# Two 32-byte paddings in SBUF: the moving operands of a matmul stream shifted against its weights

## The reference, cut to what matters

```python
p  = rmsnorm(x, norm_mix) @ w_in            # first block, then its three mixers
x  = x + concat([y_a, y_b, y_c]) @ w_out
up = dwconv3(rmsnorm(x, norm_ffn) @ ffn_w_up)
x  = x + (silu(gate) * val) @ ffn_w_down    # gate, val: the halves of up
proj = rms_norm(x, norm_g) @ w_in_2         # second block, then its three branches
mk, mv = split(rms_norm(mem) @ w_mem_kv)
merged = sigmoid(ga)*(ya @ w_up_a) + sigmoid(gb)*(yb @ w_up_b) + sigmoid(gc)*(yc @ w_up_c)
out = x + merged @ w_o
```

## The kernel before, in words

| tile | bytes from raw0 | modulo 128 before |
|---|---|---|
| raw, w_hi, w_lo (12 buffers of 4096) | 0 to 49151 | 0 |
| x (16384), par (2548), con (4368) | 49152, 65536, 68096 | 0 |
| h_hi, h_lo (16384 each) | 72480, 88864 | 32 |
| shared area | 105248 | 32 |

## Time and profile before

### The profile page before, as it was taken

The page is one execution under the profiler, slowest core; times in us unless marked ns, Lnnn a source line. Parts: engine busy times, 40 slices in busy tenths (PEclk is TensorE's granted clock), DMA queues, the critical chain, the costliest instruction groups (busy, mean ns, idle before and its releaser), DMA issues.

```text
span 2505.9 us, 51128 instructions
## 1 busy us (share of the span) xinstructions
PE 2418.7 (97%) x19960; PEld 2378.8 (95%) x19960; DVE 1533.2 (61%) x2050; ACT 1186.3 (47%) x1502; POOL 12.8 (1%) x27
## 2 busy tenths in 40 slices
PE   6999998999999999996899999999999999999999
PEld 6899998999999999996899999999999999999999
DVE  6556566666556666567866666776576454544454
ACT  5343335666435666434444445444465443433433
POOL 0000000000000000000000000000000000000000
PEclk9999898999999999998999999999999999999999
DMA  6353354555555555553333333333344365555554
GB/s 236 136 186 118 132 187 136 183 189 179 201 187 179 183 191 180 197 187 128 122 118 112 112 112 120 120 115 118 139 161 160 117 202 177 186 177 173 189 185 159
DMA packets 110145, 400.39 MB, mean 160 GB/s; under 512 B 12394, under 2 KB 12421, under 8 KB 109904
## 3 DMA queue, kind: packets, MB, share of 16 engines
q1 hardware_dynamic: 108000, 391.00, 46.7%
q0 software_dynamic: 2032, 7.67, 0.9%
HBM read 396.52 MB, written 2.10 MB: 159 GB/s over the span
## 4 chain that ended last, share of the span: by engine, by line
PE 91%; DVE 5%; issue 1%; ACT 1%; DMA 0%; DVEq 0%; SPq 0%; ACTq 0%
PE bank L417 90%; DVE w_lo L1316 1%; DVE scratch L1365 1%; ACT w_hi L909 1%; PE bank L611 1%; DVE h_lo L1362 0%; DVE s_k L1365 0%; DMA x<-in_xT 0%; DVE cum L1362 0%; DVE root L1404 0%; DVE ping L1362 0%; DVE s_t L1362 0%; DVE qr L1807 0%; DVE acc L1362 0%; DVE s_t L1369 0%
## 5 line engine op out<-in xcount | busy, mean ns | idle before, releaser
L1316 DVE TENSOR_TENSOR w_lo<-raw,w_hi 128x1024 fp32r<-128x1024 f32 x736 | 891.7, 1224 | 775.2 <-ACT w_hi L909 766.8
L909 ACT ACTIVATE w_hi<-raw 128x1024 fp32r<-128x1024 f32 x736 | 771.1, 1058 | 987.2 <-PE bank L417 966.9
L417 PE MATMUL bank<-h_hi,w_hi 128*128 128x256 f32 x4016 | 1151.1, 287 | 38.0 <-DVE h_lo L1362 15.9
L417 PE MATMUL bank<-h_lo,w_hi 128*128 128x256 f32 x4016 | 1128.2, 281 | 0.0
L417 PE MATMUL bank<-h_hi,w_lo 128*128 128x256 f32 x4016 | 1127.4, 281 | 0.0
L417 PEld LDWEIGHTS bank<-h_hi,w_hi 128*128 128x128 f32 x4016 | 762.5, 190 | 48.4 <-issue 22.4
L417 PEld LDWEIGHTS bank<-h_lo,w_hi 128*128 128x128 f32 x4016 | 762.6, 190 | 3.0 <-issue 1.9
L417 PEld LDWEIGHTS bank<-h_hi,w_lo 128*128 128x128 f32 x4016 | 761.8, 190 | 0.0
L417 PE MATMUL bank<-m_hi,w_hi 128*128 128x256 f32 x704 | 196.5, 279 | 0.0
L417 PE MATMUL bank<-m_lo,w_hi 128*128 128x256 f32 x704 | 196.5, 279 | 0.0
L417 PE MATMUL bank<-m_hi,w_lo 128*128 128x256 f32 x704 | 196.5, 279 | 0.0
(11 more groups left out here) (414 smaller groups left out, 2815.8 us busy)
## 6 DMA issues: line engine op xcount, KB each, us to landing
raw<-in_units SPq DMA_DIRECT2D x736, 512.0 KB, 3.4
x<-in_xT SPq DMA_DIRECT2D x4, 512.0 KB, 6.3
memx<-in_memT POOLq DMA_DIRECT2D x4, 512.0 KB, 7.0
out_y<-obuf SPq DMA_DIRECT2D x8, 256.0 KB, 4.1
bias_t<-in_bias POOLq DMA_DIRECT2D x8, 192.0 KB, 2.9
dft<-in_dft POOLq DMA_DIRECT2D x1, 1024.0 KB, 7.4
decay<-in_decay POOLq DMA_DIRECT2D x1, 768.0 KB, 5.5
con<-in_con SPq DMA_DIRECT2D x1, 546.0 KB, 8.5
```

The costliest lines, as they stand in the source:

```text
L417: return pe.matmul(out, lhsT, rhs, start=start, stop=stop, skip_group_check=True)
L909: return act.activation(out, in_, ACT.Copy, scale=scale)
L1316: dve.tensor_tensor(w_lo[slot][:, :, :], raw[slot][:, :, :], w_hi[slot][:, :, :].bitcast(F32), ALU.subtract).then_inc(split_done, 1)
```

## The change

Two tiles of 32 bytes that nobody reads or writes are allocated, one ahead of `h_hi` and one ahead of the shared area. `h_hi` and `h_lo` move up by 32 bytes, and everything in the shared area moves up by 64. `spare` is placed 768 bytes lower in the shared area, since behind it no room for the shift is left. By the sizes above, the h pair then starts at 72512 bytes, 64 modulo 128, and the shared area at 105312 bytes, 96 modulo 128; the weights, x, par and con stay. No instruction is added or taken away.

```diff
         con = sb("con", [P, NCONST])
+        sb("pad_h", [P, 8])
         h_hi = sb("h_hi", [P, KT, T], F32R)
         h_lo = sb("h_lo", [P, KT, T], F32R)
+        sb("pad_arena", [P, 8])
         arena_at = nc.sbuf_base
...
         K = 1024
-        spare = place("spare", [P, 8], 105 * K)
+        spare = place("spare", [P, 8], 106752)
```

## The result

The changed kernel takes 2526.84 us (2522.24 to 2535.75, 7 runs) against 2510.84 us (2504.41 to 2513.36, 7 runs) for the kernel before: ratio 1.0082, 95% interval 1.0065 to 1.0099. It is slower by 0.8%, which is 16 us between the medians and 21 by the ratio. The profiled executions differ by 2525.59 - 2507.54 = 18.05 us.

What follows compares the result with a forecast made beforehand. The prediction took the pace of TensorE's matmul stream to bound the kernel. Its terms, 0 + 0 + 0 and the two paces, gave 2507 us, own range 2500 to 2520, and 2496 to 2556 for 8 in 10.

Steps and rivals of the forecast that it cites:

- What bounds the kernel: Whole kernel: the pace of TensorE's matmul stream sets the time, with 91% of the chain on TensorE.
- Instructions, transfers, vector engines at 0: All queues, weight loads and conversions: nothing added or moved that costs time, 0, bound ±1.3 us for the vector engines.
- the remark that at half clock the distance does not matter: Matmuls at half clock: about 200 ns each, so a load of 188 ns fits inside whatever the distance.
- The matmul stream at 0 ns per matmul: All float32r matmuls: new distances between moving operand and weights cost 0 ns, bounds -5 and +3 ns, -86 to +52 us.
- the slower rival: Matmul stream: 64 or 96 is a worse distance, 3 ns per matmul, 2559 us, area alone 2524; chance 0.17.
- The first, full-float32 matmuls at two distances with equal times: Full-float32 matmuls of 256 columns: 215.5 ns at distance 32 and 215.2 at 0, taken as no effect, weak evidence.
- The second, the 3 ns between chains of 128 columns and transposes: Load-limited chains: 112 ns at distance 0, transposes 109 at 96; the difference need not be the distance.
- The third, regularity over steps of 512 bytes: Matmul stream: distances change in multiples of 512 bytes, yet all come at 116.7 or 117.7 ns.
- The small difference is not one of addresses: Feed-forward windows: paces 116.7 and 117.7 ns occur in the same loop at the same addresses, so addresses do not cause them.
- The faster rival: Matmul stream: 32 bytes is a bad distance costing some 5 ns; avoiding it gives 2421, 2447 or 2479 us; chance 0.15.
- Two read ports: TensorE: independent read ports for moving operand and weights, from a skill page; by it the sum is also 0.
- 109.2 ns: Matmul stream: a skill page's estimate for 256 columns, N / 2.4 + 2.5 ns, against 116.7 in the trace; 2378 us.

Runs made afterwards that it cites:

- all_up32: The kernel before with 32 bytes of padding ahead of the first buffer, so weights and everything behind move up by 32: ratio 0.9994, 2505.73 us.
- h448_a448: The change's two paddings at other sizes, h and the shared area both at 448 modulo 512 from the weights: ratio 0.9818 to the kernel before, 2462.87 us.
- w_up96: The kernel before with w_hi and w_lo moved by 96 bytes and everything behind them by 512: ratio 0.9873, 2474.81 us.
- w_lo_up96: The kernel before with only w_lo moved by 96 bytes and what lies behind by 512: one run, 2538.47 us against 2503.27.
- h_lo_up64: The kernel before with only h_lo moved by 64 bytes, the shared area kept at 288 modulo 512: one run, 2513.96 us against 2508.75.
- short_loads: The changed kernel with 64 instead of 128 weight columns in two of three matmuls of unit(): one run, 2517.73 us.
- short_moves: The changed kernel with 128 instead of 256 moving columns in two of three matmuls of unit(): 3263.83 us.

## Why the prediction was wrong, point by point

**What bounds the kernel:** right. TensorE's stream was 91% of the chain and is 92% of it; each nanosecond per matmul appeared in the time nearly in full (20 us worked out below, 18.05 measured).

**Instructions, transfers, vector engines at 0:** right. The conversions kept 1224 and 1058 ns, and the busy times of both engines agree within 0.6 us. So was the remark that at half clock the distance does not matter (last section).

**The matmul stream at 0 ns per matmul:** this is the step that failed. The distance of moving operand and weights sets the pace, and the term is not 0. The measured terms are +3.3 ns in y and m (116.7 to 120.0), +2.3 in ya and mg (mostly 117.7 before), and for h +1.0 where it had been at 116.7, against -3.3 in a few units. As an estimate over the units of the two profiles: y and m 2880 x 3.3 = 9.5 us, ya and mg 1920 x 2.2 = 4.2, mh some 2, and h some 239 units more at 117.7 for 6 us less 25 units at 113.3 for 2. The sum is 20 us, where the profiles differ by 18.05. In y and m the term is even beyond the upper bound of +3 that the prediction set. The parts measured alone point the same way: 0.5% with the area at 96 and h untouched, 0.17% with both at 64. They do not add up to the change strictly, since the second moves the area as well; h alone at 64 was not tried.

**The numbers:** the likeliest time, 2507, and its own range of 2500 to 2520 rest on the 0. The wide range, up to 2556, takes in the measured 2526.84 only because most of the slower rival was put into it, and that rival had 0.17.

**Why the reasons for 0 did not hold.** The first, full-float32 matmuls at two distances with equal times, was called weak and was: in the profiles of eleven kernels, over which the float32r stream went from 113.3 to 120.0, `gsq,con` stayed between 215.5 and 216.0 ns. The second, the 3 ns between chains of 128 columns and transposes, was none of distance; the transposes went from 96 to 32 and stayed at 0.60 us for four. The third, regularity over steps of 512 bytes, was correct as an observation, and the prediction named the loophole itself, a conflict in the lowest bits that are constant over the stream. I gave that loophole too little. Some 5 ns lay unexplained between what the rows of parts allow and what the stream takes, and at 192 most of them go (113.3). They were the hint that the distance costs something; once it does, there is no reason for the present distance to be neutral.

**"The small difference is not one of addresses":** right, and it misled me. One place has two paces, and in the feed-forward block of all_up32 and of h448_a448 each half keeps one of them from its start to its end. That was taken as evidence against an effect of the place. But the place sets which two paces there are.

**The rivals.** The slower one came true in its place, the area, and in its size there; that load and moving read meet more often, as it says, no run shows. Its time for the area alone, 2524, is near the measured time, partly by luck, since h lost some 4 us too and the kernel before was 3.7 us above 2507 beside the changed one; its 3 ns for every matmul, 2559, is what h at 96 and the area at 0 came near to (2548.87). The faster rival was wrong for this change and right for its neighbours: with both at 192 modulo 256 the stream gains 3.3 ns per matmul where it draws the quick pace, 2462.87 us, and the rival gave 2421 to 2479.

**Two read ports, and 109.2 ns.** The section "Who interferes with whom" of the Trainium skill's page "SBUF — State Buffer" has the two read ports of TensorE independent and nothing but the port shared by VectorE and GpSimd as a source of contention. For the time, the runs disagree: moving the weights alone by 96 bytes took 1.3% off the kernel (w_up96). They do not show that it is the ports that clash. The 109.2 ns that the prediction worked out from "Back-to-back issue gap" (the Trainium skill, "TensorE: Matmul & The Clock Gate") was reached at no distance; the best was 113.3. The section gives that formula for matmuls taken alone, without the loads of a stream.

**What stays open.** That the relative place of moving operand and weights sets the pace is shown. How it does is not. An average over the matmuls' own distances fails in w_lo_up96 and is doubtful in h_lo_up64. Shorter reads took the y stage from 120.0 to 113.3, shorter loads only to 117.7, and nothing brought it below 113.3. What draws one of two paces at the start of a stretch is not shown either, nor why 64 modulo 256 mostly draws the slow one and 192 mostly the quick one. Steps under 32 bytes were not tried.

## What to carry to other kernels

Where a stream of matmuls with a weight load each sets the time, try a few paddings of 32 bytes between moving operands and weights, over a period of at least 256 bytes; here they span 0.982 to 1.016 of the time, with no instruction changed. Move both weight buffers alike, and all moving operands of the stream (the one run that moved the low weights alone was slower than either distance by itself), and measure several runs, since one place can have two paces. If a pace lies above what its parts allow and nothing waits, treat addresses as a suspect, however regular the trace is.

## What the runs showed of the hardware that was not expected

**The pace comes in steps, and only at full clock.** At half clock three such matmuls take 640 ns, as in the kernel before:

```profile
390.30 0.41 PE L417 MATMUL bank<-h_hi,w_hi 128*128 128x256 f32 x1
...
390.94 0.41 PE L417 MATMUL bank<-h_hi,w_hi 128*128 128x256 f32 x1
```

That is 213.3 ns each, and it is the same 640 at all eight distances of the table. The distance costs nothing there. It is also the same with two of three loads cut (short_loads) and with two of three reads cut (short_moves). So 213.3 / 2 = 106.7 ns is a fair estimate of what the full clock would give if nothing but the clock counted. The shortest pace found is 113.3 and the longest 120.0, one and two times 6.7 ns above it. Those between are repeating cycles of gaps: in the kernel before 113, 116, 117, 120 ns and again, 466.7 for four, which is 6 steps in four matmuls. Whether the first step of 6.7 ns has the same cause as the second is not shown.

**A busy stream can stay at half clock.** In short_moves, with the moving reads of two matmuls in three cut to 128 columns, the granted clock falls to 1.2 GHz where TensorE pauses ahead of the up-projection, as it does in the changed kernel. There it is full again by 395.9 us, in the first units of the up-projection. In short_moves TensorE is then busy without a break for 450 us, and the clock stays at half until the down-projection, whose reads are full (TensorE's columns alone):

```profile
320.00:405.00 85.00, 85.00 (x753) 1.00 0.59 194
405.60:419.00 13.40, 2.08 (x5) 0.67 0.26 80
420.00:870.00 450.00, 450.00 (x2112) 0.50 0.31 101
875.00:998.00 123.00, 123.00 (x1027) 1.00 0.55 181
```

The first line is the same cut stream in the w_out stage, which began at full clock and kept it. Over that run the mean is 0.742, against 0.984 in short_loads, where only the loads were shortened. At half clock a triple takes 0.64 us with the cut reads as with the full ones, so reading a third less saved nothing there, and the lower clock made the kernel 30% slower than the kernel before.
